# Key and query norms with tokens on partitions, and a reordered delta-rule stage with the inversion in one orientation

## The chip, the cores and the metric

The kernel runs on one core of one Trainium2 chip. The metric is the device time of one execution in microseconds (us), the median of several executions. The core has five engines that work side by side: TensorE (PE in the profile) for matrix products, VectorE (DVE), ScalarE (ACT), GpSimd (POOL) and SyncE (SP), which here only issues weight loads. Products are written to PSUM, which has eight banks of 128 x 512 fp32 numbers; DVE and ACT read them there.

## The reference

Two layers of a trunk run for a prompt of 256 tokens and for 8 samples of one token, 264 columns in all. Each layer has a mixer (an S5 state-space branch and a gated DeltaNet branch) and a channel sub-layer (SwiGLU in layer 0, 8 experts in layer 1). The change lies in the DeltaNet branch (4 heads of 128):

```python
qkv_c, conv_new = causal_conv(qkv, conv0, w)            # silu at its end
q = l2norm(q.reshape(nb, L, H, 128)); k = l2norm(k.reshape(nb, L, H, 128))
# l2norm(x) = x * rsqrt(sum(x * x, -1) + 1e-6)
g = -exp(a_log) * softplus(a_lg + dt_bias); beta = sigmoid(b_lg)
...
gc = cumsum(g); decay = where(tril, exp(gc_i - gc_j), 0)
lower = where(strict, (k * beta) @ k.T * decay, 0)
sol = triangular_solve(lower + eye, [v * beta, k * beta * exp(gc)])
attn = where(tril, q @ k.T * decay, 0)
...
# per chunk, with the state S
v_new = u - w @ S;  o = (q * exp(gc)) @ S + attn @ v_new
S = S * exp(gc_last) + (k * exp(gc_last - gc)).T @ v_new
```

The samples take one step of the same recurrence each, from states that are loaded.

## The kernel before

Features lie on partitions and the 264 tokens along the free axis. PE's order is written out by hand; weights stream through a ring of seven 512 KB slots, loaded by SP. A "unit" is one piece of independent work on one such slot: u below 16 is a projection for the merge gates (`project`, 8 fp32 products of 128x128 by 128x264, which the profile shows as 16 instructions), from 16 on a pair of GLU projections with 4 products each. Each layer has 24 units. A slot of the modulation weights (`ada_slots`) gives two products of 32x128 by 128x512, as four instructions; 16 slots in each layer are spread over the DeltaNet stage (`LATE`).

The mixer first computes the S5 branch and the q/k/v projections, with DVE busy on the scans and the convolution, and then the DeltaNet stage with two chunks of 128 prompt tokens (c = 0, 1). `fill(step)` puts units and slots between the steps of that stage, as many as `UNITS` and `LATE` say; PE, ACT and DVE each call it at their own places, ACT for the sigmoid of a unit, DVE for the multiplication of a GLU unit. `batch4` is a step of 4 products of 128x128, one for each head, into one bank: 8 instructions if it is a product and 4 if it is a transpose. `open_bank` takes the seven banks in rotation and waits until the readers of the bank's last content have given it back, so a reader that is late stops PE seven banks later. `takes` and `taken` wait for that.

The steps around the change, in PE's order:

1. `fill(0)`: 4 units; `s5_y` of the last tile; 4 modulation slots.
2. `qkn`: after ACT has squared q and k (L1086), 8 products with a matrix of ones (L541) sum the squares over the partitions and spread the sum to all of them, 128x264 each. DVE adds EPS (L1609), ACT takes the root of 128x2112 numbers (L1097), DVE the reciprocal (L1612), and scales q and k (L1615, L1616).
3. `gcc` and `gcb` (L599 and the helper line L431): cumulative sums of g. They wait for `g_done`, the last of `gdn_columns`, which needs Exp, Ln, Exp and Sigmoid on ACT (L1090 to L1093). `fill(2)`: 4 units, 6 slots.
4. After `qk_done`: `ktok` (transposes, L606), `kk` and `qk`; DVE forms the masked and decayed matrices `ln`, `att`, `kg`, `kbg`, `qg`. `fill(3)`: 2 units.
5. `lt` and `vtok` (transposes, L613, L614), masks on DVE, `fill(4)`: 2 units, 2 slots.
6. The inverse of I + lower. First inside blocks of 16: three times e and eT are squared (`e`, `eT`, copied out by ACT at L1120) and the inverse p and its transpose pT are both multiplied and added (`p`, `pT`, L1685). Then three levels (`yl`, `x`, `xT`) join the blocks.
7. `wt`, then for each chunk `vn`, `o`, `s` (L664, L676).
8. The samples: DVE prepares `dg` and `sx` (L1717 to L1722), PE does `skt` (L687), `sgb`, `sqk`; 2 units, 4 slots; then `skq`, 32 products of a loaded state of 128x128 by 2 columns (L703). The states come by a 2 MB load that ACT issues (L1148) when the prompt's state, which lay in the same place, has been written out. DVE, `svt` (L709), 2 units; DVE spreads the result (L1743) and decays the state (L1747); `so` (L716), 8 products of 512 columns.
9. The norm of the output (`on`, L549; DVE L1758, L1763 to L1765), 3 units, then the projections `go` and `wo`.

The DeltaNet stage of layer 0 begins at 157.4 us of the profile, that of layer 1 at 801.1 us. Layer 0's channel sub-layer lies between them, and the experts take the time from 1061.9 us to the end.

## Time and profile before

| | us |
|---|---|
| median of 3 runs (lowest to highest) | 2139.69 (2136.61 to 2140.27) |
| the profiled execution's own time | 2137.92 |
| its span, first to last instruction | 2136.1 |
| PE busy | 2016.4 |
| DVE busy | 1578.8 |
| ACT busy | 1080.0 |

The mean granted clock of TensorE is 0.958 of full speed. The page divides the span into 40 slices of 53.4 us; PE is busy for 8 or 9 tenths of nearly all. "Idle before" in a row is the time for which the engine stood still just before an instruction, and what ended it. The rows are those of one profiled execution, on core 0, in us from the span's start. "L431" is the helper line of all `batch4` products that `one` makes, L272 that of all products with ring weights, L1322 and L1328 those of DVE's `tt` and `ts`.

### The profile page before, as it was taken

The numbers are of one execution on the slowest core, as the hardware profiler recorded it, in microseconds if no ns is written. First come the engines' busy times: TensorE is split into PE (matmuls) and PEld (weight loads), VectorE is DVE, ScalarE is ACT, GpSimd is POOL, SyncE is SP. The second block draws the span as 40 slices with busy tenths as digits, with TensorE's granted clock in tenths as the row PEclk, the third lists the DMA queues.
The fourth block names the chain that finished last, engine by engine and source line by source line (L and its number), as shares of the span: only waits on it lengthen the run. The fifth ranks groups of instructions, "written<-read, shape, count | busy, mean of one in ns | idle before, by whom it ended". The sixth has DMA issues, their size and how long they took to land.

```text
span 2136.1 us, 29895 instructions
## 1 busy us (share of the span) xinstructions
PE 2016.4 (94%) x11258; PEld 1675.9 (78%) x11258; DVE 1578.8 (74%) x2188; ACT 1080.0 (51%) x1308; POOL 133.9 (6%) x232
## 2 busy tenths in 40 slices
PE   7998999799998998899899999999999999999996
PEld 4776887699998876887778788787887877888784
DVE  6884526455565694626489998999989999899986
ACT  2124211245433114211268777777777777677773
POOL 3440000000002440000000000000000000000000
PEclk9999997999999999998989999999999999999998
DMA  8575233455553454224449999999989999999992
GB/s 334 192 265 187 83 122 135 153 193 183 177 167 100 143 178 166 102 104 147 143 156 373 360 348 321 341 366 348 366 326 336 369 345 354 322 353 371 338 345 99
DMA packets 142328, 523.88 MB, mean 245 GB/s; under 512 B 16112, under 2 KB 16624, under 8 KB 141424
## 3 DMA queue, kind: packets, MB, share of 16 engines
q1 hardware_dynamic: 140112, 508.82, 66.7%
q10 hardware_dynamic: 1440, 7.90, 0.9%
q0 software_dynamic: 640, 5.35, 0.7%
q8 instruction: 86, 1.41, 0.3%
q14 instruction: 50, 0.41, 0.1%
HBM read 515.57 MB, written 6.43 MB: 244 GB/s over the span
## 4 chain that ended last, share of the span: by engine, by line
PE 78%; DVE 14%; ACT 4%; issue 2%; POOL 2%; DMA 1%; ACTq 0%; DVEq 0%
PE bank L863 25%; PE bank L889 14%; PE bank L272 14%; PE bank L729 11%; PE bank L431 4%; DVE wlo L2018 3%; DVE arena L1322 2%; PE bank L810 1%; DVE arena L1612 1%; ACT whi L1165 1%; PE bank L850 1%; DVE slab L1556 1%; PE bank L703 1%; PE bank L716 1%; PE bank L447 1%
## 5 line engine op out<-in xcount | busy, mean ns | idle before, releaser
L2018 DVE TENSOR_TENSOR wlo<-ring,whi 128x1024 fp32r<-128x1024 f32 x756 | 910.4, 1222 | 164.3 <-ACT whi L1165 158.4
L1165 ACT ACTIVATE whi<-ring 128x1024 fp32r<-128x1024 f32 x756 | 799.4, 1059 | 315.5 <-PE bank L863 151.5
L272 PE MATMUL bank<-hT,ring 128*128 128x264 f32 x1408 | 335.4, 399 | 11.8 <-ACT hT L1013 5.1
L272 PEld LDWEIGHTS bank<-hT,ring 128*128 128x128 f32 x1408 | 275.1, 197 | 67.9 <-issue 15.2
L863 PE MATMUL bank<-whi,gh 128*128 128x512 f32 x896 | 285.8, 400 | 3.1 <-DVE wlo L2018 2.3
L863 PE MATMUL bank<-whi,gl 128*128 128x512 f32 x896 | 279.6, 393 | 0.0
L863 PE MATMUL bank<-wlo,gh 128*128 128x512 f32 x896 | 278.7, 392 | 0.0
L863 PEld LDWEIGHTS bank<-wlo,gh 128*128 128x128 f32 x896 | 168.2, 188 | 39.2
L863 PEld LDWEIGHTS bank<-whi,gl 128*128 128x128 f32 x896 | 168.0, 188 | 37.9
L863 PEld LDWEIGHTS bank<-whi,gh 128*128 128x128 f32 x896 | 161.1, 188 | 36.9 <-DVE wlo L2018 5.6
L889 PE MATMUL bank<-whi,eh 128*128 128x512 f32 x448 | 142.3, 399 | 3.2 <-DVE wlo L2018 3.2
L889 PE MATMUL bank<-wlo,eh 128*128 128x512 f32 x448 | 141.2, 396 | 0.0
L889 PE MATMUL bank<-whi,el 128*128 128x512 f32 x448 | 141.1, 396 | 0.0
L729 PE MATMUL bank<-hh,whi 128*128 128x264 f32 x448 | 128.2, 286 | 11.2 <-DVE hl L2026 11.2
L729 PE MATMUL bank<-hh,wlo 128*128 128x264 f32 x448 | 127.8, 285 | 0.0
L729 PE MATMUL bank<-hl,whi 128*128 128x264 f32 x448 | 127.7, 285 | 0.0
L889 PEld LDWEIGHTS bank<-whi,el 128*128 128x128 f32 x448 | 84.5, 189 | 20.4
L889 PEld LDWEIGHTS bank<-wlo,eh 128*128 128x128 f32 x448 | 84.3, 188 | 20.6
L889 PEld LDWEIGHTS bank<-whi,eh 128*128 128x128 f32 x448 | 82.3, 188 | 23.0 <-DVE wlo L2018 4.9
L729 PEld LDWEIGHTS bank<-hh,whi 128*128 128x128 f32 x448 | 85.3, 190 | 11.6 <-issue 11.6
L431 PEld LDWEIGHTS bank<-arena 128*128 128x128 f32 x704 | 83.8, 198 | 7.3 <-issue 6.7
L431 PE MATMUL bank<-arena 128*128 128x128 f32 x704 | 85.1, 283 | 4.7 <-issue 4.7
(368 smaller groups left out, 2474.8 us busy)
## 6 DMA issues: line engine op xcount, KB each, us to landing
ring<-in_w SPq DMA_DIRECT2D x964, 512.0 KB, 5.2
arena<-in_gdn ACTq DMA_DIRECT2D x2, 2048.0 KB, 8.2
out_gdns<-arena POOLq DMA_DIRECT2D x2, 2048.0 KB, 8.1
xT<-in_x ACTq DMA_DIRECT2D x1, 1056.0 KB, 9.0
out_y<-hT SPq DMA_DIRECT2D x1, 1056.0 KB, 3.9
masks<-in_masks ACTq DMA_DIRECT2D x1, 512.0 KB, 11.1
cpk<-in_cpk SPq DMA_DIRECT2D x1, 512.0 KB, 6.7
bt<-in_bt SPq DMA_DIRECT2D x1, 512.0 KB, 7.0
```

Of the source, the lines that this page charges most:

```text
L272: ins = pe.matmul(out, w, rhs, start=start, stop=stop)
L431: return lambda o, h: pe.matmul(o, a(h), b(h), start=True, stop=True)
L447: ins = pe.matmul(bank[7][32 * j:32 * j + 32, :], cT[:, at // 2, :], ring[:, i, 512 * jj:512 * jj + 512], start=at // 2 == 0, stop=at // 2 ...
L703: ins = pe.matmul(ps[:, 2 * i:2 * i + 2], s0[:, i, :], cv[:, h:h + NH + 1:NH, SEQ + b], start=True, stop=True)
L716: close(pe.matmul(ps[:, :], ktk[:, :], vm[0:hb, 4 * i:4 * i + 4, :].rearrange("p a b -> p (a b)"), start=True, stop=True), name)
L729: ins = pe.matmul(o, w, x, start=first and n == 0, stop=last and n == 2)
L810: ins = pe.matmul(bank[2 * (i % 2) + part][:, PAIR * (m % 2):PAIR * (m % 2) + PAIR], src[:, t, m * P:(m + 1) * P], dsel[:, t, :], start=t ...
L863: ins = pe.matmul(o[half], x[:, k, mine], w[part][:, CH * half:CH * half + CH], start=k == 0 and n == 0, stop=k == KD - 1 and n == 2)
L889: ins = pe.matmul(bank[6 + half][0:CAP, :], x[:, s, :], w[part][:, CH * half:CH * half + CH], start=s == 0 and n == 0, stop=s == FT - 1 an ...
L1165: act.activation(whi[:, m % SPL, :], ring[:, r, :], ACT.Copy).then_inc(sem("hi_done"), 1)
L1322: d(v.tensor_tensor(o, a, b, op))
L2018: v.tensor_tensor(wlo[:, m % SPL, :], ring[:, (low.base + m) % RING, :], whi[:, m % SPL, :].bitcast(F32), ALU.subtract).then_inc(sem("lo_d ...
```

## The change

Eight things are done:

- The sums of squares are formed with tokens on partitions: 24 products whose stationary operand is a piece of the squares (128 features by 128 tokens, or by the 8 samples) and whose moving operand is one column of ones. The result is 128x24 (`qn`) in one bank. EPS, root and reciprocal work on 128x24.
- The factors are spread over the partitions by products whose stationary operand is one column of `qn`, broadcast, with the unit matrix as moving operand: `rk` and `rq` (a `batch4` for each chunk), and `rs` for the samples. DVE multiplies k and q with the banks, the keys first.
- `kk` comes right after the keys; `ln` is made at once, its negation folded into one instruction; `ktok`, `qk`, and the masks of `att` follow.
- ACT squares q and k before the GELUs, in another place of the arena, after the last scan has come back (`s_back`). The four small activations for g and beta move to the fourth q/k/v projection, Exp twice in a row, and `gdn_columns` to the middle of the S5 steps.
- In the squaring stage only pT is carried; the third `eT` goes; p comes from two batches of transposes at the end (`p`, `fill("turn")`).
- `samples_in` (the preparation of `dg` and `sx`) goes from behind the last state to before the masks.
- Units are placed otherwise. Before: 4, 1, 4 (with 6 slots), 2, 2 (with 2 slots) up to the squaring stage, none in it; 3 in the levels; then 1, 2, 2, 3. After: 3, 1, 1 (4 slots), 1 (2 slots), 2 (2 slots), and 2 at the end of the squaring stage; 4 in the levels, 1 after `wt`, 1 and 1 in the chunks, 2, 1, 1, 3 with the samples. The order of the weights in HBM follows.
- The turn of the late modulation and its reading on DVE come before `svt`; one unit lies before it and one behind.

```diff
-UNITS = [4, 1, 4, 2, 2] + [0] * 7 + [1] * 3 + [0] * 4 + [1, 2, 2, 3]
-LATE = {0: 4, 2: 6, 4: 2, 20: 4}
+UNITS = {"y": 3, "norm": 1, "k": 1, "ln": 1, "e": 2, "sq0": 0, "pr0": 0, "sq1": 0, "pr1": 0, "sq2": 0, "pr2": 1, "turn": 1,
+         "yl0": 0, "x0": 1, "yl1": 1, "x1": 1, "yl2": 0, "x2": 1, "wt": 1, "vn0": 1, "vn1": 1, "skq": 2, "svt": 1,
+         "so": 1, "on": 3}
+LATE = {"y": 4, "k": 4, "ln": 2, "e": 2, "skq": 4}
...
+        qn = sb("qn", [P, 3 * 2 * NH])
...
-        sq = ar(6 * B1, KD, N)
+        sq = ar(3 * B1, KD, N)
...
                 ada_turn(*ADA_IN[l][-1])
-                fill(0)
+                fill("y")
                 s5_y(l, UT - 1)
-                ada_slots(LATE[0])
-
-                pe.wait_ge(sem("qk_sq"), l + 1)
-                for i in range(2 * NH):
-                    ps = open_bank(pe, ("qkn", l, i))
-                    close(pe.matmul(ps[:, 0:N], ones[:, :], sq[:, i, :], start=True, stop=True), ("qkn", l, i))
-                fill(1)
+                ada_slots(LATE["y"])
                 gdn(l, fill)
...
+                pe.wait_ge(sem("qk_sq"), l + 1)
+                name = ("qkn", l)
+                ps = open_bank(pe, name)
+                for g in range(3):
+                    m = P if g < 2 else NB
+                    for i in range(2 * NH):
+                        a = 2 * NH * g + i
+                        ins = pe.matmul(ps[0:m, a:a + 1], sq[:, i, P * g:P * g + m], ones[:, 0:1], start=True, stop=True)
+                close(ins, name)
                 pe.wait_ge(sem("g_done"), l + 1)
...
-                fill(2)
-                pe.wait_ge(sem("qk_done"), l + 1)
+                fill("norm")
+
+                def spread(name, c, h0):
+                    at = 2 * NH * c + h0
+                    batch4((name, l, c), lambda o, h: pe.matmul(o, qn[:, at + h:at + h + 1].broadcast_to([P, P]), ident,
+                                                                start=True, stop=True))
+
+                pe.wait_ge(sem("qn_done"), l + 1)
+                for c in range(NC):
+                    spread("rk", c, NH)
+                fill("k")
+                for c in range(NC):
+                    taken(pe, ("rk", l, c))
+                    batch4(("kk", l, c), one(k(c), k(c)))
+                for c in range(NC):
+                    spread("rq", c, 0)
+                name = ("rs", l)
+                ps = open_bank(pe, name)
+                for i in range(2 * NH):
+                    a = 2 * NH * NC + i
+                    ins = pe.matmul(ps[:, NB * i:NB * i + NB], qn[0:NB, a:a + 1].broadcast_to([NB, P]), ident[0:NB, 0:NB],
+                                    start=True, stop=True)
+                close(ins, name)
                 for c in range(NC):
                     batch4(("ktok", l, c), lambda o, h: pe.transpose(o, k(c)(h), ident))
                 for c in range(NC):
-                    batch4(("kk", l, c), one(k(c), k(c)))
+                    taken(pe, ("rq", l, c))
                     batch4(("qk", l, c), one(k(c), q(c)))
-                fill(3)
+                fill("ln")
...
                         batch4(("e", l, s, c), one(at("eT", c), at("e", c)))
-                        batch4(("eT", l, s, c), one(at("e", c), at("eT", c)))
-                    fill(5 + 2 * s)
+                        if s < 2:
+                            batch4(("eT", l, s, c), one(at("e", c), at("eT", c)))
+                    fill(f"sq{s}")
                     for c in range(NC):
                         taken(pe, ("e", l, s, c))
-                        taken(pe, ("eT", l, s, c))
                         if s:
                             taken(pe, ("pT", l, s - 1, c))
-                        batch4(("p", l, s, c), one(at("eT", c), at("p", c)))
                         batch4(("pT", l, s, c), one(at("e", c), at("pT", c)))
-                    fill(6 + 2 * s)
+                    fill(f"pr{s}")
+                for c in range(NC):
+                    taken(pe, ("pT", l, 2, c))
+                    batch4(("p", l, c), lambda o, h: pe.transpose(o, mats["pT"][c][:, h, :], ident))
+                fill("turn")
...
                 close(ins, name)
+                ada_turn(*ADA_LATE[l])
+                fill("svt")
                 pe.wait_ge(sem("svn_done"), l + 1)
                 name = ("svt", l)
                 ps = open_bank(pe, name)
                 close(pe.transpose(ps[0:hb, 0:P], sx[:, 1, 0:hb], ident), name)
-                ada_turn(*ADA_LATE[l])
-                fill(21)
+                fill("so")
                 pe.wait_ge(sem("vm_done"), l + 1)
...
+                    if m == UT + 3:
+                        act.wait_ge(sem("ax_done"), l + 1)
+                        then(act, act.activation(gd[:, 1, :], gd[:, 1, :], ACT.Exp, scale=-1.0), "a_gd")
+                        act.activation(gd[:, 3, 0:NH], col(l, "a_log"), ACT.Exp).then_inc(sem("a_ln"), 1)
+                        act.activation(gd[:, 1, :], gd[:, 1, :], ACT.Ln, bias=1.0).then_inc(sem("a_ln"), 1)
+                        act.activation(gd[:, 4, :], gd[:, 4, :], ACT.Sigmoid).then_inc(sem("a_ln"), 1)
...
+                act.wait_ge(sem("s_back"), JT // 2 * (l + 1))
+                act.activation(sq, cv[:, 0:2 * NH, :], ACT.Square).then_inc(sem("qk_sq"), 1)
                 for i in range(UT):
                     if i == UT - 1:
-                        fill(0)
+                        fill("y")
                     act.wait_ge(sem("y_sum"), UT * l + i + 1)
                     act.activation(uT[:, i, :], uT[:, i, :], ACT.Gelu_apprx_tanh).then_inc(sem("gelu_done"), 1)
-                act.activation(sq, cv[:, 0:2 * NH, :], ACT.Square).then_inc(sem("qk_sq"), 1)
...
+            def qk_sums(l):
+
+                if l == 0:
+                    d(v.memset(qn[:, :], 1.0))
+                name = ("qkn", l)
+                ps, n = filled(v, name), 2 * NH * NC
+                d(v.tensor_scalar(qn[:, 0:n], ps[:, 0:n], EPS, None, ALU.add))
+                takes(v, v.tensor_scalar(qn[0:NB, n:], ps[0:NB, n:n + 2 * NH], EPS, None, ALU.add), name)
+                v.tensor_copy(ini[:, 3:4], qn[:, 0:1]).then_inc(sem("nrm_ss"), 1)
+
+            def qk_roots(l):
+
                 v.wait_ge(sem("nrm_root"), l + 1)
-                d(v.reciprocal(nrm[:, :, :], nrm[:, :, :]))
-                q, k = cv[:, 0:NH, :], cv[:, NH:2 * NH, :]
-                v.wait_ge(sem("cv_silu"), 3 * (l + 1))
-                d(v.scalar_tensor_tensor(q, q, HD ** -0.5, nrm[:, 0:NH, :], ALU.mult, ALU.mult))
-                v.tensor_tensor(k, k, nrm[:, NH:2 * NH, :], ALU.mult).then_inc(sem("qk_done"), 1)
-                v.wait_ge(sem("qk_done"), l + 1)
+                d(v.reciprocal(qn[:, :], qn[:, :]))
+                q = qn[:, :].rearrange("p (g i) -> p g i", i=2 * NH)[:, :, 0:NH]
+                v.tensor_scalar(q, q, HD ** -0.5, None, ALU.mult).then_inc(sem("qn_done"), 1)
+
+            def scaled(l, name, c, h0):
+
+                ps = filled(v, (name, l, c))[:, :].rearrange("p (h t) -> p h t", h=NH)
+                x = cv[:, h0:h0 + NH, P * c:P * c + P]
+                takes(v, v.tensor_tensor(x, x, ps, ALU.mult), (name, l, c))
+
+            def samples_in(l):
+
+                name = ("rs", l)
+                ps = filled(v, name)[:, 0:2 * NH * NB].rearrange("p (h b) -> p h b", b=NB)
+                x = cv[:, 0:2 * NH, SEQ:N]
+                takes(v, v.tensor_tensor(x, x, ps, ALU.mult), name)
...
+                v.tensor_tensor(dg[:, 1], bc(gd[0:NB, 4, 8:12, None], W), idb, ALU.mult).then_inc(sem("dg_done"), 1)
...
+                v.tensor_tensor(r(sx[:, 0, 0:NH * NB]), q, k, ALU.mult).then_inc(sem("qkp_done"), 1)
...
+                    if c == 0:
+                        qk_roots(l)
                 v.wait_ge(sem("a_col"), 2 * (l + 1))
...
                 for c in range(NC):
+                    scaled(l, "rk", c, NH)
+                for c in range(NC):
                     v.wait_ge(sem("a_dec"), 2 * NC * l + 2 * c + 2)
-                    tt(mats["decT"][c], mats["decT"][c], bc(upper[:, None, :], H4), ALU.mult)
                     tt(mats["dec"][c], mats["dec"][c], bc(strict[:, None, :], H4), ALU.mult)
                     tt(mats["dec"][c], mats["dec"][c], bc(c4(4, c)[:, :, None], H4), ALU.mult)
+                    name = ("kk", l, c)
+                    ps = filled(v, name)[:, :].rearrange("p (h t) -> p h t", h=NH)
+                    ins = v.scalar_tensor_tensor(mats["ln"][c], ps, -1.0, mats["dec"][c], ALU.mult, ALU.mult)
+                    takes(v, ins, name)
+                    v.tensor_copy(ini[:, 3:4], mats["ln"][c][:, 0, 0:1]).then_inc(sem("ln_done"), 1)
+                for c in range(NC):
+                    scaled(l, "rq", c, 0)
+                samples_in(l)
+                for c in range(NC):
+                    tt(mats["decT"][c], mats["decT"][c], bc(upper[:, None, :], H4), ALU.mult)
                     name = ("ktok", l, c)
...
+                    if j == S5_STEPS // 2:
+                        gdn_columns(l)
```

## Rows read from the trace of the kernel before

**Rows 1.** The head of the page and its busy times.
```profile
span 2136.1 us, 29895 instructions
PE 2016.4 (94%) x11258; PEld 1675.9 (78%) x11258; DVE 1578.8 (74%) x2188; ACT 1080.0 (51%) x1308; POOL 133.9 (6%) x232
```

**Rows 2.** Windows: stretch, length, PE busy (instructions), clock, DMA share, GB/s.
```profile
184.00:190.00 6.00, 6.00 (x25) 0.75 0.28 87
209.00:220.00 11.00, 6.33 (x39) 0.69 0.65 257
220.00:237.00 17.00, 17.00 (x92) 1.00 0.40 124
261.30:268.60 7.30, 7.29 (x50) 0.77 0.01 2
306.00:315.50 9.50, 9.50 (x40) 0.82 0.80 310
317.20:328.30 11.10, 11.09 (x68) 0.63 0.56 190
345.00:352.50 7.50, 7.50 (x14) 0.50 0.24 103
704.90:713.40 8.50, 8.40 (x183) 0.76 0.02 4
853.00:864.70 11.70, 7.11 (x41) 0.71 0.62 239
```

**Rows 3.** Waits of PE, 150 to 407: total, times, longest.
```profile
PE bank L541 <- DVE arena L1609: 3.9, 1, 3.9
PE bank L606 <- ACT arena L1109: 3.8, 1, 3.8
PE bank L431 <- issue: 2.3, 1, 2.3
PE bank L687 <- DVE sx L1722: 2.3, 1, 2.3
...
PE bank L664 <- DVE arena L1706: 1.1, 1, 1.1
...
PE bank L431 <- ACT arena L1109: 0.4, 1, 0.4
```

**Rows 4.** The chain in layer 0: start, length, what, instructions.
```profile
153.38 1.85 PE bank L447 x16
...
157.37 14.24 PE bank L272 x64
...
215.42 4.94 PE bank L431 x32
...
227.48 0.44 PE bank L613 x4
...
237.35 21.64 PE bank L431 x192
```

**Rows 5.** Timeline: two token-logit products and the norms' reciprocal.
```profile
51.70 4.09 PE L381 MATMUL bank<-wab,hT 128*128 128x8 f32 x47
...
193.13 13.35 DVE L1612 RECIPROCAL arena<-arena 128x2112 f32<-128x2112 f32 x1 [6.30 <-ACT arena L1097]
...
1061.95 7.45 PE L381 MATMUL bank<-wr,hT 128*128 128x8 f32 x48 [7.78 <-ACT hT L1013]
```

**Rows 6.** Timeline of the sample part of layer 0.
```profile
307.45 0.33 ACTq L1148 DMA_DIRECT2D arena<-in_gdn  x1
...
317.17 11.12 PE L703 MATMUL bank<-slab,arena 128*128 128x2 f32 x64
...
329.69 4.41 DVE L1743 TENSOR_TENSOR arena<-bank,masks 32x4096 f32<-32x4096 f32 x1
...
354.42 6.75 DVE L1763 RECIPROCAL hT<-hT 128x1056 f32<-128x1056 f32 x1 [1.15 <-ACT hT L1157]
```

**Rows 7.** The source view of line 1148, its last line.
```profile
DMA to landing us min/median/max: 8.1/8.2/8.4
```

More of the change, by code:

```diff
@@ L340, in units @@
         def units(step):
-            return range(sum(UNITS[:step]), sum(UNITS[:step + 1]))
+            steps = list(UNITS)
+            at = sum(UNITS[s] for s in steps[:steps.index(step)])
+            return range(at, at + UNITS[step])
         def ada_ends(l):
@@ L1109, in mixer @@
                     gives(act.activation(mats["qg"][c], ps[:, :].rearrange("p (h t) -> p h t", h=NH), ACT.Exp), name)
-                fill(3)
-                fill(4)
+                for step in ("norm", "k", "ln", "e"):
+                    fill(step)
                 for s in range(3):
                     if s:
-                        fill(4 + 2 * s)
+                        fill(f"pr{s - 1}")
                     for c in range(NC):
-                        for n in ("e", "eT"):
+                        for n in ("e", "eT") if s < 2 else ("e",):
                             name = (n, l, s, c)
-                            filled(act, ("eT", l, s, c))
+                            filled(act, ("eT" if s < 2 else "e", l, s, c))
                             ps = filled(act, name)
                             gives(act.activation(mats[n][c], ps[:, :].rearrange("p (h t) -> p h t", h=NH), ACT.Copy), name)
-                    fill(5 + 2 * s)
+                    fill(f"sq{s}")
+                for step in ("pr2", "turn"):
+                    fill(step)
                 for s in range(3):
-                    fill(10 + 2 * s)
+                    if s:
+                        fill(f"x{s - 1}")
                     for c in range(NC):
@@ L1148, in mixer @@
                 act.dma_start(s0, gdn_in[l]).then_inc(sem("s0_in"), 16)
-                fill(20)
+                fill("skq")
                 ada_copy(ADAS.index(ADA_LATE[l]) + 1)
-                fill(21)
+                for step in ("svt", "so"):
+                    fill(step)
                 act.wait_ge(sem("os_done"), l + 1)
@@ L2262, in layouts @@
         fills, late, at = np.concatenate([w[UT + S5_STEPS:], glu], axis=0), ada(*ADA_LATE[l]), 0
-        for step, n in enumerate(UNITS):
-            k = sum(UNITS[:step])
+        k = 0
+        for step, n in UNITS.items():
             m = LATE.get(step, 0)
             parts += [fills[k:k + n], late[at:at + m]]
-            at += m
+            k, at = k + n, at + m
         parts += [_slots(_flat(_blocks(i["w_gdn_out"][l]))), _slots(_flat(_blocks(i["w_out"][l])))]
```

104 lines of the change are left out of this document (37 added, 67 removed).

## The prediction

> **What bounds the kernel now.** I read the head of the page first: PE is busy for 94% of the span [rows 1]. So a gain must either take work off PE or close its gaps. The chain of waits says the same inside the changed stage: it is nearly all PE, unit after unit and batch after batch [rows 4]. Then the waits of PE in layer 0's stage: ten rows, from 3.9 us to 0.4 us, 18.1 us together, of which 10.7 us lie ahead of the inversion (3.9, 3.8, 1.5, 1.1 and 0.4), 2.3 us between its squaring part and its levels, and 5.1 us behind [rows 3]. Last the windows, for the clock: after a gap PE often works at the lower of its two levels (1.2 GHz, 0.5 in the column) for some us. The stretch with two gaps before `kk` has a granted clock of 0.69, in layer 1 0.71; the one behind the 2.3 us gap 0.77, the ones behind and around the sample part 0.82, 0.63 and 0.50 [rows 2]. A gap so costs more than its length. DVE, though its reciprocal of the norms takes 13.35 us [rows 5], is hidden there by four units and six slots; what it costs is only what PE waits.
>
> **Prices.** A unit is 14.24 / 4 = 3.56 us, a slot of modulation weights 1.85 / 4 = 0.46 us, a batch of transposes 0.44 us, a `batch4` product 21.64 / 24 = 0.90 us, and one of its instructions 0.113 us [rows 4]. Each of the 16 instructions of the old `qkn` has a unit's shape, so they cost 3.56 us.
>
> The new `qkn` (24 products, 48 instructions) isn't in the trace. The nearest row is `L381`: also 24 products with 128, 128 and 8 columns of weights, and a moving operand of 8 columns. It took 4.09 us at the full level, and 7.45 us after a long gap [rows 5]. I take 4.1, since PE comes to it from four units' worth of full work, and keep 7.45 for the range. `rk` and `rq` are four batches with a broadcast stationary operand, the form of `gcb`: 4 x 0.90 = 3.6 us. `rs` has 16 instructions with 128 columns of weights: 16 x 0.113 = 1.8 us, or 2.8 us at the 11.1 / 64 = 0.173 us of `L703` [rows 6]. I take 1.8.
>
> **Up to the squaring stage.** From the first unit at 157.37 to 237.35 us [rows 4] are 80.0 us. At full clock the work before is 13 units 46.3, 12 slots 5.6, `s5_y` about 1.5 (157.37 - 155.2 less the turn), `qkn` 3.6, `gcc` and `gcb` 2.1, `ktok` 0.9, `kk` and `qk` 3.6, `lt` and `vtok` 1.8: 65.4 us. With 10.7 us of gaps, 3.9 us are left, and these are the lower level: `kk` and `qk` alone took 4.94 instead of 3.6 us [rows 4]. After: 8 units 28.5, 12 slots 5.6, 1.5, new `qkn` 4.1, 2.1, spreads 3.6, `rs` 1.8, `ktok` 0.9, `kk` and `qk` 3.6, 1.8: 53.5 us. The five units that move back are 17.8 us, so work alone has grown by 5.9 us, and the gaps decide. I followed them in order:
>
> - `g_done`: its four activations now run during the fourth q/k/v projection, where ACT only waits for PE; three table changes and the rest are some 5 us, beside projections of 3.56 us each with seven banks between. `gdn_columns` adds 0.8 us to DVE in the middle of the S5 steps, in a stretch in which PE no longer waits for it. Free; if that cover were gone, 0.8 us a layer and up to 5 us for ACT. Both gaps before 190 us (5.4 us) go, as `sq` is ready before `s5_y`.
> - Norms: after the last small product DVE adds EPS (0.6 us), ACT roots beside it, DVE reads `gcc` and `gcb` (seven small ones, 1.4), forms the first differences (1.55), then inverts 24 columns (at 13.35 / 2112 = 6.3 ns each 0.15, some 0.45 with the multiplication). `gcb` lands 2.1 us behind `qkn`, so `qn_done` is there at 2.1 + 1.4 + 1.55 + 0.45 = 5.5 us; PE's cover is 2.1 + 3.56 = 5.7 us. No gap, with 0.2 us to spare.
> - Keys: DVE needs 0.7 us for each chunk, under one unit and four slots (5.4 us). `kk` waits for nothing. `ln` is out 2 us before `ktok` ends. The scaled queries are ready some 1 us before PE comes to `qk`.
> - Masks: DVE has 5 x 0.7 for each chunk, then 5 x 0.7 each for `lt` and `vtok`; it ends `e_done` about 2.6 us before PE is through with units `ln` and `e`.
> - Banks: `rq` of chunk 1 needs the bank of the unit `norm`, which ACT reads only after its six exponentials; that is 5 us earlier than needed.
>
> So the 10.7 us go and most of the 3.9 us: 80.0 - 17.8 - 53.5 = 8.7 us. I leave 0.5 us for gaps and 0.8 us for the lower level behind the small products, since a similar crowd of small products has a clock of 0.76 over 8.5 us in layer 1 [rows 2], which is 2 us lost, and take **7.4 us**.
>
> **Squaring.** Before: 24 batches, 21.64 us without a gap, then 2.3 us [rows 3, 4]. After: 5 batches a chunk for e and eT and 3 for pT, 16 x 0.90 = 14.4 us, and two batches of transposes, 0.9 us. With no unit between, each step now leans on ACT's copies (0.55 us each, two a chunk) of the other chunk: the copy of chunk 1's e lands 0.1 us before its `pT` could start, in all three rounds. I give 0.4 us for that. Unit `pr2` covers the last additions, unit `turn` the copies of p and the first masks (2.8 us), so the 2.3 us go. 24.0 - 15.3 - 0.4 = **8.3 us**. The levels behind it had a clock of 0.77 over 7.3 us [rows 2]: **1.7 us** back. The 0.7 us before `o` goes under the unit `vn0`; the 1.1 us before the second `vn` stays [rows 3]: **0.7 us**.
>
> **Samples.** `samples_in` takes away the 2.3 us before `skt` [rows 3] and the 0.82 behind it, 9.5 x 0.18 = 1.7 us [rows 2]. What is late next is the state: its load is issued at 307.45 us and lands 8.2 us later, at 315.65 [rows 6, 7]. PE came to `skq` at 317.17; without gap and slow clock it comes at 313.2 and waits 2.5 us. Behind `skq`, `svt` no longer waits for DVE (1 us), but only one unit of 3.56 us covers the 4.41 us of `L1743` [rows 6] and the GLU unit that DVE now does first: 2 us of gap, and `so` starts nearer to the lower level. The end goes by the output norm (6.75 us of reciprocal and its neighbours), unchanged. I take this tail as even and the part as 2.3 + 1.7 - 2.5 + 1 - 2 = **0.5 us**, with -3 and +4 as bounds, the 0.50 over 7.5 us [rows 2] being 3.7 us that could come back or stay.
>
> **Sum.** 7.4 + 8.3 + 1.7 + 0.7 + 0.5 = 18.6 us a layer; layer 1 repeats layer 0 [rows 2]: 37.2 us. Nothing behind the stage holds it back: the channel parts start when the mixer ends. The profiled execution took 2137.9 us (span 2136.1), which becomes 2100.7; it lies 1.8 us below the median, so the median would be 2102.5. I say 2102.
>
> **A rule and a row.** Transposes lie in a full stretch with clock 1.00: the window of 220 to 237 us holds four batches of them [rows 2]. The Trainium skill, "TensorE: Matmul & The Clock Gate", Part 4 (PE-mode transpose), says that a transpose doesn't count as PE work for the clock as a product does. By that, `rs` with `ktok` behind it, and the transposes of p, would be short rests; the sum would be some 3 us smaller, about 2105; by the row it stays.
>
> **Rivals.**
> 1. *The short covers don't hold.* The norm chain has 0.2 us to spare, the queries 1, the squaring 0.1. If each handover is some tenths longer, PE stands 2 to 3 us before `rk` and `kk` and 2 us in the squaring, with a lower clock behind as in rows 2: 8 to 9 us less a layer, 2119. For it: three margins under 1 us. Against: the gaps seen now are long waits, not handovers. 0.18.
> 2. *More comes back than counted.* Without gaps the lower level also leaves the sample part (0.63, 0.50) and the tail: 6 us more a layer, 2090. Against: `L703` itself is at the lower level with no gap before it. 0.13.
> 3. *Slower: the clock.* 24 products with one column, broadcasts and transposes are little for the array. If PE stays at the lower level from `qkn` to `qk`, that stretch of 27 us (4.1 + 2.1 + two units 7.1 + 1.9 + spreads 3.6 + `rs` 1.8 + 0.9 + 3.6, and handovers) takes 54: 2102 + 2 x 27 = 2156. It decides from 18.6 us of work a layer at the lower level, two thirds of that stretch. Against: `L381` ran at 4.09 us, and units of full width lie between. 0.03.
> 4. *No change,* if the gaps come back in full elsewhere (the state's load and `vm`) : 2138. Against: these are behind 17 us of savings that no wait takes back. 0.02.
>
> My forecast has 0.64, and its own range is 2094 to 2111. The likeliest time is 2102; the range must reach into rivals 1 and 2: 2087 to 2120. A change of 0.2% is 4 us, about what a measurement of this kernel can tell from none. Faster 0.95, same 0.02, slower 0.03.
>
> **What would show it.** PE's waits for L1609, L1109 and `issue` gone, none above 1 us before the squaring; squaring in 15 to 16 us without units; the clock there at 1.00; a wait of about 2.5 us at `skq` for the load; `qkn` near 4 us. It is wrong if `qkn` takes over 7 us or the windows up to the levels show a clock under 0.8.

## The result and the profile after

The changed kernel takes 2121.57 us (median of 5 runs, 2117.86 to 2126.57); the kernel before, run beside it, 2139.69 us (5 runs). The ratio is 0.9922 with a 95% interval of 0.9902 to 0.9942: faster, by 18.1 us, where the forecast was 2102 us, 37 us faster. The time lies outside the range of 2087 to 2120. The profiled execution is the median one, with a span of 2119.8 us against 2136.1 [rows 1].

The head of the page:

```profile
span 2119.8 us, 29948 instructions
...
PE 2015.4 (95%) x11306; PEld 1676.2 (79%) x11306; DVE 1534.9 (72%) x2171; ACT 1069.6 (50%) x1300; POOL 134.2 (6%) x232
```

PE is as busy as before, 2015.4 against 2016.4 us, in a span 16.3 us shorter: on balance the gaps alone have shrunk. Line numbers have moved: `qkn` is now L601, `skt` L718, `skq` L734, `svt` L742, `so` L748, units L274, `batch4` L435, slots L451, the state's load L1181, the write-out of the prompt's state L2203. PE's waits in layer 0's stage, 150 to 401 us:

```profile
PE bank L734 <- DMA arena<-in_gdn: 6.6, 1, 6.6
PE bank L748 <- DVE ini L1802: 2.3, 1, 2.3
PE bank L695 <- DVE arena L1767: 1.1, 1, 1.1
PE bank L274 <- DVE slab L1820: 0.6, 1, 0.6
PE bank L274 <- DVE sx L1792: 0.2, 1, 0.2
```

Of the ten waits of [rows 3] only the 1.1 us before the second `vn` is left in its place. Two long ones have come: 6.6 us for the load of the samples' state (7.1 us in layer 1), which is now the longest, and 2.3 us before `so`. The windows, with the columns of [rows 2] (busy time of PE, PEld, DVE, ACT and POOL, then clock, DMA share and GB/s): ahead of `kk`; from the spreads to the last unit before the squaring; squaring with its two units; levels and chunks; `skq`; `so` and output norm. The last row is layer 1's counterpart of the first.

```profile
177.30:185.60 8.30, 8.30 (x34) 7.44 (x35) 4.38 (x17) 3.26 (x7) 0.00 (x0) 0.65 0.53 196
188.00:215.00 27.00, 27.00 (x178) 21.76 (x180) 20.37 (x36) 2.61 (x6) 0.00 (x0) 1.00 0.56 195
215.87:238.50 22.63, 22.63 (x172) 21.50 (x169) 6.80 (x10) 5.93 (x11) 0.00 (x0) 1.00 0.28 93
238.50:288.00 49.50, 48.45 (x321) 44.64 (x320) 11.02 (x17) 10.30 (x20) 0.00 (x0) 1.00 0.23 75
304.70:318.40 13.70, 13.70 (x65) 13.70 (x66) 0.00 (x0) 0.00 (x0) 0.00 (x0) 0.50 0.17 67
331.10:346.70 15.60, 15.58 (x25) 7.25 (x26) 11.51 (x14) 0.41 (x1) 0.54 (x1) 0.57 0.08 35
...
811.30:818.40 7.10, 7.10 (x34) 6.32 (x34) 3.49 (x17) 2.29 (x5) 0.00 (x0) 0.77 0.55 209
```

From 188 to 288 us PE works without a stop but the 1.1 us, at the full level. The clock is down once before that, ahead of `kk`, and again behind 298 us, in the sample part. The timeline of both places shows, among others, these instructions (start, length, and in brackets the idle time before):

```profile
172.71 4.27 PE L601 MATMUL bank<-ones,arena 128*128 128x1 f32 x48
...
177.36 3.76 PE L435 MATMUL bank<-masks,gd 128*128 128x128 f32 x16
180.91 4.80 PE L274 MATMUL bank<-hT,ring 128*128 128x264 f32 x16
...
288.05 0.27 PE L718 MATMUL bank<-masks,sx 128*32 128x128 f32 x1
...
289.73 0.33 SPq L952 DMA_DIRECT2D ring<-in_w  x1
...
290.15 0.54 POOL L2203 DMA_DIRECT2D out_gdnp<-arena  x1 [116.23 <-DVE ini L1875]
...
293.29 0.33 SPq L952 DMA_DIRECT2D ring<-in_w  x1
...
294.22 0.33 ACTq L1181 DMA_DIRECT2D arena<-in_gdn  x1
...
296.16 1.92 PE L451 MATMUL bank<-ring,cT 128*32 128x512 f32 x16
304.68 13.81 PE L734 MATMUL bank<-slab,arena 128*128 128x2 f32 x64 [6.60 <-DMA arena<-in_gdn]
...
331.12 11.93 PE L748 MATMUL bank<-arena,ktk 32*128 32x512 f32 x16 [2.31 <-DVE ini L1802]
```

The last lines of the source views of L2203 (the write-out) and of L1181 (the load):

```profile
DMA to landing us min/median/max: 4.0/4.2/4.3
...
DMA to landing us min/median/max: 10.4/10.5/10.6
```

Before, the write-out landed in 2.3 us and the load in 8.2 [rows 7]. In these rows the order is to be seen: a ring load (512 KB) is issued 0.4 us *ahead* of the write-out and another 0.9 us ahead of the state's load. Before, the write-out was issued at 305.13 us, the load at 307.45 [rows 6], and the first ring load of this place at 307.58, behind both. Write-out, ring load and `so` in the timeline of the kernel before, and the last line of the source view of its write-out (L2152):

```profile
305.13 0.54 POOL L2152 DMA_DIRECT2D out_gdnp<-arena  x1 [129.28 <-DVE ini L1824]
...
307.58 0.33 SPq L920 DMA_DIRECT2D ring<-in_w  x1
...
339.33 9.39 PE L716 MATMUL bank<-arena,ktk 32*128 32x512 f32 x16
...
DMA to landing us min/median/max: 2.3/2.3/2.3
```

**Where the time went.** The stage, from its first unit to the first unit of `go`, in us a layer, positive for time saved; the moved units are taken out by count at 3.56 us:

| part | forecast | layer 0 | layer 1 |
|---|---|---|---|
| up to the squaring | 7.4 | 5.2 | 7.0 |
| squaring, levels and chunks, with the gap at `skt` | 8.3 + 4.7 | 13.9 | 13.9 |
| `skt` to `go` | -1.8 | -11.7 | -13.0 |
| sum | 18.6 | 7.4 | 7.9 |

(4.7 is 1.7 for the clock, 0.7 for `o` and the 2.3 us of the gap, which the prediction booked under the samples as 0.5 = 2.3 - 1.8.) The first two parts gave 19.1 and 20.9 us of 20.4 forecast. The loss stands in the third. In it, layer 0 and layer 1: the way to `skq` 1.6 and 1.6 us shorter; the wait for the load 6.6 and 7.1; `skq` 2.6 and 3.1 longer; from there to `so` 1.7 and 1.9 longer, its new gap within; `so` to `go` 2.4 and 2.6 longer, nearly all of it in `so` (11.93 us, before 9.39).

### The profile page after: what moved, and what is told of

Its sections match the earlier page's. It is cut to its first block, busy times and chain, and to the rows that moved or that the text cites. A ratio compares the mean times of both kernels' runs of the same rounds, so it can differ in the third digit from the quotient of the medians.

```text
span 2119.8 us, 29948 instructions
## 1 busy us (share of the span) xinstructions
PE 2015.4 (95%) x11306; PEld 1676.2 (79%) x11306; DVE 1534.9 (72%) x2171; ACT 1069.6 (50%) x1300; POOL 134.2 (6%) x232
## 4 chain that ended last, share of the span: by engine, by line
PE 80%; DVE 12%; ACT 2%; DMA 2%; POOL 2%; issue 1%; ACTq 0%; DVEq 0%
PE bank L895 25%; PE bank L274 14%; PE bank L921 14%; PE bank L761 11%; PE bank L435 4%; DVE wlo L2069 3%; DVE arena L1356 2%; PE bank L842 1%; PE bank L734 1%; ACT whi L1199 1%; PE bank L882 1%; PE bank L748 1%; DVE slab L1590 1%; PE bank L451 1%; DMA arena<-in_gdn 1%
## 5 line engine op out<-in xcount | busy, mean ns | idle before, releaser
L274 PE MATMUL bank<-hT,ring 128*128 128x264 f32 x1408 | 337.2, 399 | 12.2 <-ACT hT L1045 5.1
L274 PEld LDWEIGHTS bank<-hT,ring 128*128 128x128 f32 x1408 | 274.2, 197 | 67.4 <-issue 15.2
L761 PE MATMUL bank<-hh,whi 128*128 128x264 f32 x448 | 128.5, 287 | 11.2 <-DVE hl L2077 11.2
L761 PEld LDWEIGHTS bank<-hh,wlo 128*128 128x128 f32 x448 | 85.7, 191 | 0.0
L761 PEld LDWEIGHTS bank<-hl,whi 128*128 128x128 f32 x448 | 85.3, 190 | 0.0
## 6 DMA issues: line engine op xcount, KB each, us to landing
arena<-in_gdn ACTq DMA_DIRECT2D x2, 2048.0 KB, 10.5
```

Source lines behind the costliest of these rows:

```text
L274: ins = pe.matmul(out, w, rhs, start=start, stop=stop)
L761: ins = pe.matmul(o, w, x, start=first and n == 0, stop=last and n == 2)
```

## The experiments

Theory A: the late state does it. PE comes to the two units in front of `skq` earlier, the ring loads that these set free go ahead of the write-out and of the load, both land late, and PE waits and then works through `skq` at the lower level. The rivals: the loss is due to the four slots' transfers (A1); it is the clock in the sample part, whatever the load does; or it came with the inversion or the norms. One execution's profile can't rank these. All ratios are to the kernel before, run beside each; its medians were 2140.6 us beside e1 to e4, 2139.2 beside e5 to e8 and 2140.6 beside e9 and e10.

**e1: the changed kernel, with the state loaded early.** The prompt's state gets a place of its own, so that the samples' state need not wait for its write-out.

```diff
-        s_pr = ar(5 * B1, NH, P)
+        s_pr = ar(12 * B1, NH, P)
...
                     # ACT, behind the copy of vn
+                    if c == NC - 1:
+                        act.dma_start(s0, gdn_in[l]).then_inc(sem("s0_in"), 16)
...
-                act.wait_ge(sem("sp_out"), 16 * (l + 1))
-                filled(act, ("s", l, NC - 1))
-                act.dma_start(s0, gdn_in[l]).then_inc(sem("s0_in"), 16)
...
                     # ACT, at the mixer's end
+                act.wait_ge(sem("sp_out"), 16 * (l + 1))
```

> The changed kernel with one thing altered: the prompt's state (s_pr) lies elsewhere in the arena, so ACT can issue the load of the samples' states right after it has copied vn of chunk 1, some 12 us earlier, without waiting for the prompt's state to be written out. Theory A (the load's wait before skq, 6.6 and 7.1 us in the changed kernel, is what took the missing gain, together with the lower clock that this gap leaves behind): the wait goes to 0, skq falls from 13.8 us towards the 11.1 us of before, the unit behind it from 5.5 to some 4.5; 9 to 11 us a layer, so 2099 to 2103 us. Theory B (skq, 32 products with two columns, sends the clock down in any case and the gap adds nothing to that): only the waits go, 13.7 us, 2108 us. Theory C (the load isn't the cause; PE would wait for something else at that place): under 5 us, 2117 or more.

Measured 2102.72 us (5 runs), ratio 0.982 (0.9806 to 0.9834): 18.9 us less than the changed kernel. The load's wait is gone from the waits; the timeline of the same place, load first:

```profile
282.29 0.33 ACTq L1174 DMA_DIRECT2D arena<-in_gdn  x1
...
298.28 9.99 PE L734 MATMUL bank<-slab,arena 128*128 128x2 f32 x64
...
320.87 11.96 PE L748 MATMUL bank<-arena,ktk 32*128 32x512 f32 x16 [2.31 <-DVE ini L1802]
```

The load now has 16 us before it is used and takes 8.4. `skq` falls from 13.81 to 9.99 us: the wait cost its own 6.6 us and 3.8 more in the products behind it. By the traces the part from `skt` to `go` is 10.5 and 11.3 us shorter in the two layers; the span as a whole is only 18.9 us shorter, so that some 3 us were lost elsewhere between these two profiles. `so` is as long as before this edit, so the load is not what makes it long; that it is the 2.3 us gap ahead of it, e7 shows.

**e4: the same edit on the kernel before.**

```diff
-        s_pr = ar(5 * B1, NH, P)
+        s_pr = ar(12 * B1, NH, P)
...
+                    if c == NC - 1:
+                        act.dma_start(s0, gdn_in[l]).then_inc(sem("s0_in"), 16)
```

> The kernel before with the same early load as in the first run of this call. Theory A (before the change the load landed 1.5 us before PE needed it, so it cost nothing): no change, within 2 us of 2139.7, and skq as long as before, 11 us. Rival B (the load or its traffic cost the kernel before something too): 3 us or more faster.

Measured 2140.18 us (10 runs), ratio 1.000 (0.9991 to 1.0009). An early load by itself is worth nothing: before the change PE came to `skq` 1.3 us (layer 0) and 1.6 us (layer 1) after the state had landed.

**e2: the changed kernel, with the four slots in front of `skq` moved ahead of the chunks.**

```diff
-LATE = {"y": 4, "k": 4, "ln": 2, "e": 2, "skq": 4}
+LATE = {"y": 4, "k": 4, "ln": 2, "e": 2, "wt": 4}
```

> The changed kernel with the four modulation slots before skq moved to behind wt (some 25 us earlier); the load is issued at the same point of the program. Theory A1 (the four ring loads of 512 KB that these slots release within 2 us, just when the state's load is under way, share the DMA engines with it and stretch it from 8.2 to 10.5 us): the load lands after 8.2 to 8.6 us and the write of the prompt's state before it after 2.3 instead of 4.0 us; the wait before skq falls from 6.6 to 4.5 us, 2 us a layer, 2117 us. Rival A2 (the ring loads of the units do it, which come denser now than before the change): landing stays at 10 us or more, and the wait at 6.5 us or more, 2121 us or slower.

Measured 2129.83 us (4 runs), ratio 0.9944 (0.9929 to 0.996), slower than the changed kernel. The last lines of the source views of the write-out and of the load, and the wait:

```profile
DMA to landing us min/median/max: 4.0/4.0/4.1
...
DMA to landing us min/median/max: 9.7/9.8/9.8
...
307.58 13.81 PE L734 MATMUL bank<-slab,arena 128*128 128x2 f32 x64 [7.90 <-DMA arena<-in_gdn]
```

The slots' transfers account for 0.7 us of the landing and for nothing of the write-out: A1 falls for the larger part. With them some work that hid the load has gone too, and the waits have grown by 1.3 and 0.6 us. The other 6 us of the difference are not the wait; some 2 of them lie in layer 0's `so`, which took 14.02 us behind the same gap of 2.3 us, all of it at the lower level (11.56 in layer 1). What the others are is not shown.

**e5: the changed kernel, with DVE's preparation of the samples back behind the second chunk.** This gives back the gap at `skt`; everything behind it on PE comes that much later.

```diff
     # DVE, behind the scaled queries: only the product with rs stays early
-                samples_in(l)
+                name = ("rs", l)
+                ps = filled(v, name)[:, 0:2 * NH * NB].rearrange("p (h b) -> p h b", b=NB)
+                x = cv[:, 0:2 * NH, SEQ:N]
+                takes(v, v.tensor_tensor(x, x, ps, ALU.mult), name)
...
     # DVE, ahead of its reads of skt
+                samples_in(l)      # now dg and sx alone
```

> The changed kernel, with VectorE's preparation of the samples (dg and sx for the three small products) put back where it stood before the change, behind the last reads of the second chunk; only the multiplication of the samples' keys and queries by their norms stays early. Theory A (what makes the state's load late is the unit of the dense part that TensorE reaches 2.3 us sooner, since the gap ahead of skt is gone: its ring load is then in flight ahead of the write-out of the state and of the load): the gap of some 2.3 us at skt comes back, the write-out again takes about 2.3 us, the load lands in about 8.2 us, TensorE waits 0 to 1 us for it in place of 6.6 and 7.1, and skq takes about 11 us in place of 13.8. Time 2121.6 + 2 x 2.3 - 13 - 2 x 2.7 = about 2108 us. Rival A2 (something else that the change brought makes the load late): the landing stays at 10 us or more, the gap comes on top of it or is taken from the wait, time 2121 to 2126 us.

Measured 2111.33 us (4 runs), ratio 0.987 (0.9852 to 0.9889): 10.2 us less than the changed kernel, though PE stands 2.3 us more at `skt`. Write-out, ring load, state's load and `skq` in its timeline, then the last lines of the source views of L2203 and L1181:

```profile
285.56 0.54 POOL L2203 DMA_DIRECT2D out_gdnp<-arena  x1 [114.86 <-DVE ini L1875]
...
287.63 0.33 SPq L952 DMA_DIRECT2D ring<-in_w  x1
287.88 0.33 ACTq L1181 DMA_DIRECT2D arena<-in_gdn  x1
...
297.60 10.66 PE L734 MATMUL bank<-slab,arena 128*128 128x2 f32 x64
...
DMA to landing us min/median/max: 2.3/2.3/2.3
...
DMA to landing us min/median/max: 8.1/8.2/8.3
```

The write-out goes 2.1 us ahead of the ring load again, and both times are those of before. The state now lands 10.4 us after the write-out's issue in place of 14.5, and PE comes to `skq` 12.0 us after it in place of 7.9: the two halves, some 4 us each, turn a wait of 6.6 us into a margin of 1.7. So closing the gap at `skt`, for which the prediction counted a gain of 1.5 us even after the wait (2.3 + 1.7 - 2.5), is what cost 10 us here.

**e3: the kernel before, with the inversion of the change alone.**

```diff
-                        batch4(("eT", l, s, c), one(at("e", c), at("eT", c)))
+                        if s < 2:
+                            batch4(("eT", l, s, c), one(at("e", c), at("eT", c)))
...
-                        batch4(("p", l, s, c), one(at("eT", c), at("p", c)))
...
+                for c in range(NC):
+                    taken(pe, ("pT", l, 2, c))
+                    batch4(("p", l, c), lambda o, h: pe.transpose(o, mats["pT"][c][:, h, :], ident))
```

> The kernel before with one part of the change alone: in the squaring stage only pT is carried, the third eT goes, p comes from transposes; units, norms and the sample part as before. The forecast's step was 8.3 us a layer with two units under the tail. Without units there the tail is bare: the last additions (0.7), the transposes, two copies of p and two masks (2.8 us) before yl. Theory A: squaring 15 to 16 us without a gap inside, then 3 to 4 us of gaps around the transposes in place of 2.3, so 24.0 - 15.4 - 3.5 = 5 us a layer, of which the clock behind the gaps takes up to 1: 8 to 10 us in all, 2130 us, and the sample part unchanged, with no wait for the load. Rival B (without the second orientation the copies of ACT are waited for in each round): gaps of 0.5 us or more inside the squaring, 0 to 4 us in all.

Measured 2127.48 us (4 runs), ratio 0.9934 (0.9917 to 0.995).

```profile
240.13 14.79 PE L431 MATMUL bank<-arena 128*128 128x128 f32 x128
...
258.06 7.22 PE L431 MATMUL bank<-arena 128*128 128x128 f32 x48 [1.62 <-issue]
```

The batches take 14.79 us, as in the changed kernel; with no unit behind them, 1.6 us of gap stay ahead of the levels, so that 13.1 us are gained where 8 to 10 were expected. There is no wait for the load.

**e9: the changed kernel, with the old inversion and the late preparation of e5, so the norms without the inversion.** What else the change brought, the placing of the units and the activations moved earlier, stays in.

```diff
     # e5, and the lines of e3 taken back:
-                        if s < 2:
-                            batch4(("eT", l, s, c), one(at("e", c), at("eT", c)))
+                        batch4(("eT", l, s, c), one(at("e", c), at("eT", c)))
...
+                        batch4(("p", l, s, c), one(at("eT", c), at("p", c)))
```

> The changed kernel with the norms' part alone: the inversion again squares and multiplies in both orientations, and the samples' preparation stands behind the second chunk's last reads, as before the change (the multiplication by the norms stays early). Theory (the parts add up, and nothing but the load's lateness is missing in the changed kernel): the version with both parts and the late preparation took 2111.3 us and the inversion alone 2127.5 of 2139.5, so that the norms are worth 2139.5 - 2111.3 - 12.0 = 16.2 us and this kernel takes 2123 us, with no wait for the state's load. Up to the squaring it saves 5 to 7 us a layer, and some 2 us in layer 0 are lost ahead of it. Rival (the norms alone bring the lateness too, since they hand TensorE to the samples earlier): a wait of 2 to 7 us for the load and 2130 us or more.

Measured 2126.8 us (5 runs), ratio 0.9938 (0.9924 to 0.9952). PE waits 0.5 and 0.2 us for the load:

```profile
PE bank L732 <- DMA arena<-in_gdn: 0.5, 1, 0.5
...
309.67 12.13 PE L732 MATMUL bank<-slab,arena 128*128 128x2 f32 x64 [0.48 <-DMA arena<-in_gdn]
```

The norms with the rest are worth 13.8 us and the inversion 13.1 us, together 26.9, and e5, which has both, saves 27.9: they add up. The norms came out 2.4 us smaller than the expectation worked out, and 1.0 us smaller if each kernel is taken against the one before that ran beside it (27.9 - 13.1 = 14.8). The late load belongs to neither: the write-out landed in 2.3 to 2.7 us; the load in 8.1 us in layer 0, though in 9.9 in layer 1, where PE still waited 0.2 us only.

**e10: the changed kernel, with each small product of `qkn` issued twice.**

```diff
                         ins = pe.matmul(ps[0:m, a:a + 1], sq[:, i, P * g:P * g + m], ones[:, 0:1], start=True, stop=True)
+                        ins = pe.matmul(ps[0:m, a:a + 1], sq[:, i, P * g:P * g + m], ones[:, 0:1], start=True, stop=True)
```

> The changed kernel with each of the 24 small products of qkn issued twice, the second over the first. It prices them and what they do to the clock of the work behind them. If they cost their own time alone: qkn 8.4 in place of 4.2 us a layer, and all behind it the same: 2121.6 + 8.4 = 2130 us. If the clock behind them pays too (gcb behind them took 3.6 to 3.8 us at a lower granted clock and the unit behind that up to 4.8): gcb and the unit lose 1 to 3 us more a layer, 2132 to 2136 us.

Measured 2138.41 us (10 runs), ratio 0.9985 (0.9974 to 0.9995): 16.8 us more than the changed kernel, outside both expectations. The timeline shows the small products, first copy L601 and second L602, at two paces, and then `gcc` (L607) and the unit behind `gcb`:

```profile
176.40 0.36 PE L602 MATMUL bank<-ones,arena 128*128 128x1 f32 x2
176.62 0.36 PE L601 MATMUL bank<-ones,arena 128*128 128x1 f32 x2
...
180.30 0.57 PE L601 MATMUL bank<-ones,arena 128*128 128x1 f32 x2
180.73 0.56 PE L602 MATMUL bank<-ones,arena 128*128 128x1 f32 x2
...
187.22 0.60 PE L607 MATMUL bank<-gd,masks 128*128 128x8 f32 x2
...
191.08 3.73 PE L274 MATMUL bank<-hT,ring 128*128 128x264 f32 x16
```

From 174.81 to 187.22 us are 12.4 us for twice the work of 4.2 (11.1 in layer 1), which makes up 15 of the 16.8 us: the steps are 0.22 us at first and 0.43 us from about 177.4 us on, where the clock (0.56 in the window of 176 to 186 us) is at its lower level. The unit behind is back at 3.73 us, where it took 4.80 in the changed kernel. In both kernels `gcb` behind them is slow (3.76 us in the changed one, 187.67 to 191.08 us here, 2.03 us before the change). So the small products do bring the lower level; with 24 of them it falls on `gcb` and the unit, with 48 on themselves and `gcb`.

**e6, e7 and e8: the sample part rearranged, on e1.** e6 parts `skq` by a unit and puts the slots behind it; e7 puts two units behind `svt` and none before; e8 does both.

```diff
     # e6 and e8, PE in gdn_samples
-                fill("skq")
+                a, b2 = units("skq")
+                unit(a)
...
                 for h in range(NH):
+                    if h == NH // 2:
+                        unit(b2)
...
                 close(ins, name)
+                ada_slots(LATE["skq"])
...
     # e7 and e8, UNITS
-         ... "skq": 2, "svt": 1, "so": 1, "on": 3}
+         ... "skq": 2, "svt": 0, "so": 2, "on": 3}
```

> The changed kernel with the early load (2102.7 us), and the 32 products of skq, which read two columns each, parted by a unit: one unit ahead of the first 16, one between, and the four slots of the modulation behind the second 16, where the units and slots all stood ahead of skq. Theory C (the clock falls because of the long row of small products, 9.99 us in that version with 0.81 and 0.50 granted towards its end, and the work behind them pays for it): no stretch of small products is longer than 5 us, skq takes 2 x 4 to 4.5 us, the unit behind it 3.6 in place of 5.4, some 2 to 4 us a layer less: 2095 to 2099 us. Rival D (the clock falls whenever small products stand there, cut or not): skq the same 10 us or more and the unit between them at a lower level too: 2102 us or slower.

> The changed kernel with the early load, and the unit that stood between skq and svt put behind svt, beside the one that is there. VectorE then gets sx from skq while TensorE waits ahead of svt, and vm while TensorE works on two units. Theory: the wait of 2.3 us ahead of so goes, about 1 us comes ahead of svt (VectorE's work from skq to sx less the modulation's turn), so 1 to 1.5 us a layer less: 2100 us. Rival: with the wait moved next to skq the clock stays lower for longer and both units run slowly: 2102 us or more.

> Both edits together: skq in two parts with a unit between and the four slots behind it, and two units behind svt. The slots (1.9 us) stand now where TensorE would have waited for sx, so that nothing of the 2.3 us is left before so and next to nothing before svt. If both theories hold: 2 x (3 + 2.3) us less than 2102.7, about 2092 us. If only the waits go and the clock does not care: 2098 us. If the longer stretch of waiting VectorE work comes up elsewhere: 2102 us.

| kernel | median us (runs) | ratio, interval | against e1 |
|---|---|---|---|
| e6 | 2105.29 (4) | 0.9844, 0.9827 to 0.9861 | +2.6 |
| e7 | 2091.54 (4) | 0.9772, 0.9753 to 0.979 | -11.2 |
| e8 | 2091.8 (5) | 0.9782, 0.9764 to 0.98 | -10.9 |

e7 is the larger success, and more than the expectation counted (2100 us). Two rows of its timeline:

```profile
311.56 8.29 PE L274 MATMUL bank<-uT,ring 128*128 128x264 f32 x32
319.79 10.15 PE L748 MATMUL bank<-arena,ktk 32*128 32x512 f32 x16
```

The 2.3 us before `so` are gone, `so` takes 10.15 and 9.15 us in place of 11.96 and 11.63, and only 0.3 us came ahead of `svt`. The medians give 5.6 us a layer; by the traces the part from `skt` to `go` is 4.2 and 5.4 us shorter than in e1. With what `so` and the units around lost to the clock, the gap had so cost about twice its length or more.

e6 is undecided by its own test. In layer 1 it did what Theory C says, in layer 0 what Rival D says; its windows over the two halves, the unit between and the slots behind, first layer 0, then layer 1:

```profile
293.28:312.04 18.76, 18.76 (x97) 14.40 (x95) 2.87 (x10) 0.78 (x2) 0.00 (x0) 0.66 0.17 54
921.98:934.59 12.61, 12.61 (x97) 10.57 (x95) 2.87 (x10) 0.78 (x2) 0.00 (x0) 1.00 0.20 71
```

The same 97 instructions took 18.8 us at 0.66 in one layer and 12.6 us at 1.00 in the other. On e7 the split adds nothing that 4 and 5 runs can tell (2091.54 and 2091.8); e8 met the 2092 us of its expectation, but not by the sum given there, over half of which was the split's. e7 is the version to keep: 48 us below the kernel before and 30 us below the changed one.

## Why the prediction was wrong

The direction and the mechanisms of the gain were right; the term of the samples was mis-sized by 10 to 11 us a layer, and that put the time outside the range. In the order of its steps:

- **Up to the squaring, 7.4 us: 5.2 and 7.0.** PE's waits for L1609, L1109 and `issue` are gone, and there is none before the squaring; `qkn` took 4.27 us against 4.1 forecast. The 0.8 us that were set aside for the lower level were too few: 0.77 over 7.1 us is 1.6 us in layer 1, 0.65 over 8.3 us is 2.9 us in layer 0. The row that the prediction names for it had already shown 2 us. The 0.5 us kept for gaps, of which none came, made up for part. e10 confirms the source: it is the crowd of small products. One of the prediction's own signs of being wrong, a clock under 0.8 in a window up to the levels, was so seen, but it cost 0.4 and 2.2 us only.
- **Squaring, 8.3 us, levels 1.7, `o` 0.7:** 15.5 us without units against 15.7 forecast, clock 1.00 throughout. Right.
- **Samples, 0.5 us: this is the step that failed.** It reads "its load is issued at 307.45 us and lands 8.2 us later, at 315.65", and lets PE wait 2.5 us. Both durations, the 2.3 us of the write-out that stands in front of the load and the 8.2 us of the load, were carried over from a trace in which the ring load was issued behind both (305.13, 307.45, 307.58 us); that PE's earlier arrival would put it in front was not asked. PE's way was forecast well: from the write-out's issue to `skq` it has 7.9 us (290.15 to 298.1), and 8.1 by the prediction's own numbers (313.2 less 305.13). But write-out and load took 4.0 + 10.4 us with the handover, 14.5 in place of 10.5. These 4.0 us are the difference between a wait of 2.5 and one of 6.6.
- **What hung on it.** The prediction says that a gap costs more than its length, but it counted the 2.5 us at `skq` at their length. Behind the 6.6 us PE went through all of `skq` at the lower level, 2.6 and 3.1 us more (e1: 9.99 us without the wait). The 2.3 us before `so` were seen (2 us, less 1 us at `svt`), but "I take this tail as even" wasn't right: `so` lost another 2.4 us; in e7, without the gap, it is 1.8 and 2.5 us shorter than in e1. In layer 0 the misses add up: 4.1 for the wait, 2.6 for `skq`, 0.7 from there to `so` and 2.4 for `so` are 9.8 of the 9.9 us between -1.8 and -11.7.
- **Rivals.** Rival 1 gave 2119 us, nearest to what came, but for gaps before `rk`, `kk` and in the squaring; there are none, so its number was right by chance. The cause lay with the place that rival 4 names, "the state's load", which was held for too small to matter because the savings ahead were 17 us. They did outweigh it, but 11.7 of 19.1 us and 13.0 of 20.9 were taken back.
- **The rule on transposes.** The window with `rs` and `ktok` and that with the squaring and the first transposes of p both show 1.00. By the Trainium skill, "TensorE: Matmul & The Clock Gate", Part 4, these would have been rests; among products, as they stand here, the trace shows no fall behind them, and the row was the better guide.

What ranks the causes is the experiments: the load alone is worth 18.9 us (e1), its order and PE's later arrival together 10.2 us although 2 x 2.3 us of gap come back (e5), and the gap before `so` 11.2 us (e7). That the write-out is slower with a ring load in flight ahead of it is seen in every kernel (the last section has the rows); e5, in which one edit puts the ring load behind it again, has 2.3 against 4.2 us. The Trainium skill, "DMA: Bandwidth & Descriptors", section "Issuing engines are not separate DMA queues", says that transfers issued by different engines run on the same 16 DMA engines and interleave. By that, SP's load bears on POOL's write-out and on ACT's load. The trace agrees for the write-out (4.2 against 2.3 us) and for the load (10.5 against 8.2), but the load isn't stretched by every transfer beside it, as the rows show.

Three things stay open. Why the state's load takes 2 us more behind a ring load that is 0.9 us ahead, and nothing more beside one that is 0.7 us ahead or 0.6 us behind, none of the runs explains (the last section has the rows). Where the clock falls in the sample part differs between two layers with the same code (e6). And the first unit of layer 0's stage starts between 155.6 and 161.1 us in profiles of kernels that are alike up to there (e5 155.6, the changed kernel 158.8, e9 161.1), so that differences of 2 us between single profiles ahead of the stage say nothing.

## What to carry to other kernels

A transfer's time to landing holds only for the company it had: when an edit brings a compute engine earlier, list which transfers it sets free, in the order in which they will now be issued, and price the one you wait for behind them. A gap that is closed in front of a late transfer can cost more than it was (e5 keeps it and is 10 us faster); move the transfer first, here by giving two tenants of a buffer their own places. With that, the kernel with the gap closed is 8.6 us faster than e5; no run keeps the gap and loads early, so what closing it is then worth is not split off. And price a gap of PE with the work behind it: the 2.3 us before `so` were worth 4 to 6 us a layer.

## What the runs showed of the hardware

- What a transfer of 512 KB does to another depends on which is issued first, and by little. The pair of write-out (256 KB) and ring load was read in both layers of all twelve kernels. With the ring load 0.4 us ahead the write-out landed in 4.0 to 5.1 us (14 cases of seven kernels), with the ring load 2 us or more behind in 2.3 us (9 of 10 cases; once 2.7). The 2 MB load of the state landed in 9.7 to 10.6 us with a ring load 0.85 to 1.19 us ahead (6 cases of three kernels) and in 8.1 to 8.6 us with the nearest one between 0.68 us ahead and 0.61 behind (17 of 18 cases; once 9.9, in e9's layer 1, which nothing in the trace explains).
- Products of a 128-column stationary operand with one moving column (two instructions each) come every 0.22 us at the full level and every 0.43 us at the lower one; those with 8 stationary columns, for the samples, every 0.05 us. 16 of the first and 8 of the second (48 instructions) were through in 4.2 us and left the lower level to the work behind; of twice as many, the larger part ran at it itself.
- The same 97 instructions of e6 found the full level in one layer and the lower one in the other, 6 us apart.
